# First expert sweep of a mixture layer on Trainium2: tokens' hi and lo parts side by side as one moving operand

## What is computed

```python
def peer(h, w_q, subkeys, u, v):
    ...
        q = (xb @ w_q).reshape(PEER_BLOCK, PEER_HEADS, 2, PEER_DHALF)
        s = jnp.einsum('thpd,hpkd->thpk', q, subkeys).astype(jnp.float32)
        s1, i1 = lax.top_k(s[:, :, 0], PEER_TOPK)
        s2, i2 = lax.top_k(s[:, :, 1], PEER_TOPK)
        ...
        top, pos = lax.top_k(cand, PEER_TOPK)
        idx = jnp.take_along_axis(cidx, pos, axis=-1)
        g = jax.nn.softmax(top, axis=-1)
        ue, ve = u[idx], v[idx]
        act = jax.nn.gelu(jnp.einsum('td,thkd->thk', xb, ue).astype(jnp.float32), approximate=False)
        return jnp.einsum('thk,thkd->td', (g * act).astype(xb.dtype), ve)
```

## Time and profile before

| | us |
|---|---|
| median of 3 runs | 5239.82 |
| lowest, highest | 5237.86, 5244.24 |
| the profiled execution | 5246.08 |
| its span (first to last instruction) | 5244.1 |
| first sweep of peer00: first to last matmul into `dot` | 521.5 to 988.1 |
| the same of peer01 | 1372.5 to 1839.4 |
| the same of peer10 | 2528.4 to 2997.6 |
| TensorE busy in the whole span | 4602.8 |
| VectorE busy | 3384.8 |
| ScalarE busy | 2318.3 |
| GpSimd busy | 1137.3 |

### The profile page before, as it was taken

One profiled execution on the slowest core, in us unless ns is written; L12 is line 12 of the kernel. 1 busy time (PEld: TensorE's weight loads), 2 busy tenths in 40 slices (PEclk: granted clock), 3 DMA queues, 4 the chain that ended last, 5 costly groups with the idle time before them and its releaser, 6 DMA issues. The chain is left out here.

```text
span 5244.1 us, 91248 instructions
## 1 busy us (share of the span) xinstructions
PE 4602.8 (88%) x35718; PEld 4375.4 (83%) x35718; DVE 3384.8 (65%) x5726; ACT 2318.3 (44%) x3890; POOL 1137.3 (22%) x945
## 2 busy tenths in 40 slices
PE   8768999999899999885899999798888979888896
PEld 5546999999899999773899899698777979877796
DVE  6554797688698778725698688555365545446554
ACT  6414544455444445432454454343363434345343
POOL 0000029645105844300017745200000000000000
PEclk9888999999999999997999999899799989978898
DMA  8411686788487678620487688544314535421352
GB/s 294 163 40 46 195 278 213 233 292 297 164 256 237 217 269 296 210 101 22 158 264 224 209 288 297 186 164 150 105 53 137 184 112 174 152 93 63 135 186 94
DMA packets 293104, 950.64 MB, mean 181 GB/s; under 512 B 32592, under 2 KB 84880, under 8 KB 292038
## 3 DMA queue, kind: packets, MB, share of 16 engines
q1 hardware_dynamic: 264070, 841.59, 48.1%
q0 software_dynamic: 28032, 100.82, 5.9%
q10 hardware_dynamic: 576, 2.39, 0.1%
HBM read 899.40 MB, written 45.13 MB: 180 GB/s over the span
## 5 line engine op out<-in xcount | busy, mean ns | idle before, releaser
L150 DVE TENSOR_TENSOR weight_lo<-weight_ring,weight_hi 128x1024 fp32r<-128x1024 f32 x1420 | 1785.0, 1257 | 1295.9 <-ACT weight_hi L145 1291.1
L145 ACT ACTIVATE weight_hi<-weight_ring 128x1024 fp32r<-128x1024 f32 x1420 | 1498.8, 1056 | 1880.4 <-issue 883.7
L177 PE MATMUL ffn_gu<-second_x_hi,weight_hi 128*128 128x256 f32 x1408 | 399.3, 284 | 37.6 <-PEq L209 37.6
L177 PE MATMUL ffn_gu<-second_x_lo,weight_hi 128*128 128x256 f32 x1408 | 398.4, 283 | 0.0
L177 PE MATMUL ffn_gu<-second_x_hi,weight_lo 128*128 128x256 f32 x1408 | 398.4, 283 | 0.0
L177 PE MATMUL peer10e_dot<-peer_xh,weight_hi 128*128 128x224 f32 (+1 forms) x1152 | 325.5, 283 | 8.8 <-DVE weight_lo L150 5.9
L177 PE MATMUL peer01e_dot<-peer_xh,weight_hi 128*128 128x224 f32 (+1 forms) x1152 | 324.4, 282 | 9.2 <-DVE weight_lo L150 6.5
L177 PE MATMUL peer00e_dot<-peer_xh,weight_hi 128*128 128x224 f32 (+1 forms) x1152 | 324.3, 282 | 8.2 <-DVE weight_lo L150 5.6
L177 PE MATMUL peer10e_dot<-peer_xl,weight_hi 128*128 128x224 f32 (+1 forms) x1152 | 318.1, 276 | 0.0
L177 PE MATMUL peer10e_dot<-peer_xh,weight_lo 128*128 128x224 f32 (+1 forms) x1152 | 318.0, 276 | 0.0
L177 PE MATMUL peer00e_dot<-peer_xh,weight_lo 128*128 128x224 f32 (+1 forms) x1152 | 317.4, 275 | 0.0
(11 more groups left out here) (681 smaller groups left out, 14250.2 us busy)
## 6 DMA issues: line engine op xcount, KB each, us to landing
weight_ring<-in_peer_tiles SPq DMA_DIRECT2D x768, 512.0 KB, 4.5
weight_ring<-in_w_tiles SPq DMA_DIRECT2D x652, 512.0 KB, 3.3
peer_acts<-peer00e_gelu SPq DMA_DIRECT2D x64, 224.0 KB, 4.8
peer00e_act_in<-peer_acts SPq DMA_DIRECT2D x64, 224.0 KB, 5.3
peer_acts<-peer01e_gelu SPq DMA_DIRECT2D x64, 224.0 KB, 4.7
peer01e_act_in<-peer_acts SPq DMA_DIRECT2D x64, 224.0 KB, 5.0
peer_acts<-peer10e_gelu SPq DMA_DIRECT2D x64, 224.0 KB, 4.7
peer10e_act_in<-peer_acts SPq DMA_DIRECT2D x64, 224.0 KB, 5.2
```

The costliest lines, as they stand in the source:

```text
L145: act.activation(self.tile_of(self.hi, g), self.ring[:, g % RING, :], ACT.Copy).then_inc(self.hi_done, 2)
L150: dve.tensor_tensor(self.tile_of(self.lo, g), self.ring[:, g % RING, :], self.tile_of(self.hi, g).bitcast(F32), ALU.subtract).then_inc(sel ...
L177: last = pe.matmul(out, lhsT, rhs, start=start and i == 0, stop=stop and i == len(passes) - 1, **more)
```

## The change

The tokens' pair becomes one tensor, `x_pair[P, KD, 2, T]`, with the hi and the lo part of a k-tile next to each other. In the first sweep the two matmuls that use the hi weights become one, whose moving operand is both parts (2 x 256 or 2 x 224 columns) and whose result is 512 or 448 PSUM columns: hi by hi in the left half, lo by hi in the right half. The matmul with the lo weights adds to the left half. The two halves still have to be summed: ScalarE copies the right half out (`half`, into `q` or into a new buffer `joined`), and VectorE adds the left half to it in place (`join`). The gelu reads `joined`, in SBUF. TensorE waits before tile n for `join` of tile n-2 (`joined_done`) where it waited for ScalarE's read. The second sweep is as before.

```diff
             def score(c):
                 ...
-                pe.wait_ge(read_out, c + 1)
+                pe.wait_ge(joined_done, c + 1)
                 ...
                 if half == 0 and n >= 2:
-                    pe.wait_ge(read_out, n - 1)
+                    pe.wait_ge(joined_done, n - 1)
                 cols, width = (slice(0, T), T) if n < QT else (slice(SPARSE, T), DENSE)
                 for k in range(4):
-                    at_k = tuple(b[:, cols] for b in x(4 * half + k))
-                    last = run_passes(pe, dot[:, n % 2, 0:width], W.stationary(2 * q0 + m, k * P, at_k),
-                                      half == 0 and k == 0, half == 1 and k == 3)
+                    part = 2 * q0 + m
+                    w_hi, w_lo = (w[:, part % PARTS, k * P:(k + 1) * P] for w in (W.hi, W.lo))
+                    pe.matmul(dot[:, n % 2, 0:2 * width].rearrange("p (a t) -> p a t", a=2), w_hi, x_pair[:, 4 * half + k, :, cols],
+                              start=half == 0 and k == 0, stop=False, skip_group_check=True)
+                    last = pe.matmul(dot[:, n % 2, 0:width], w_lo, x_pair[:, 4 * half + k, 0, cols], start=False,
+                                     stop=half == 1 and k == 3, skip_group_check=True)
                 last.then_inc(W.used, 1)
...
+            def join(n):
+                dve.wait_ge(half_out, n + 1)
+                width, out = (T, q[:, n % 2, :]) if n < QT else (DENSE, joined[:, n % 2, :])
+                dve.tensor_tensor(out, out, dot[:, n % 2, 0:width], ALU.add).then_inc(joined_done, 1)
...
             for m in range(2 * front):
                 now[0] = m
+                if m % 2:
+                    join(m // 2)
                 W.next_lo(dve, 2 * q0 + m)
...
+            def half(n):
+                act.wait_ge(W.used, 2 * (q0 + n) + 2)
+                if n < QT:
+                    ...
+                    out = q[:, n % 2, :]
+                else:
+                    if n >= QT + 2:
+                        act.wait_ge(read_out, n - QT - 1)
+                    out = joined[:, n % 2, :]
+                width = out.shape[1]
+                act.activation(out, dot[:, n % 2, width:2 * width], ACT.Copy).then_inc(half_out, 1)
+
             for m in range(2 * front):
                 n = m // 2
+                if m % 2:
+                    half(n)
                 W.next_hi(act, 2 * q0 + m)
...
-                    if n < QT:
-                        if n >= 2:
-                            act.wait_ge(scored, n - 1)
-                        act.activation(q[:, n % 2, :], dot[:, n % 2, 0:T], ACT.Copy).then_inc(read_out, 1)
-                    else:
+                    if n >= QT:
                         k = (n - QT) // 2
+                        act.wait_ge(joined_done, n + 1)
                         if k >= 2:
                             act.wait_ge(stored[k % 2], 16 * (k // 2))
-                        act.activation(gelu[:, k % 2, n % 2, :], dot[:, n % 2, 0:DENSE], ACT.Gelu).then_inc(read_out, 1)
+                        act.activation(gelu[:, k % 2, n % 2, :], joined[:, n % 2, :], ACT.Gelu).then_inc(read_out, 1)
```

More of the change, by code:

```diff
@@ L704, with peer_experts @@
 LEAD = 5
-def peer_experts(nc, W, name, layer, x, route, h, gate, const, keys_dram, acts_dram, u_rows, v_rows, x_hi, x_lo, x_at):
+def peer_experts(nc, W, name, layer, x, route, h, gate, const, keys_dram, acts_dram, u_rows, v_rows, x_pair, x_at):
     q0, u0, v0 = (W.take("peer_%s%d" % (kind, layer)) for kind in "quv")
@@ L714, in peer_experts @@
     ident, iota, iota16 = const[:, 0:P], const[:, 2 * P:3 * P], const[:, 3 * P:3 * P + 16]
+    x_hi, x_lo = x_pair[:, :, 0, :], x_pair[:, :, 1, :]
     HC = PH * TOPK
@@ L755, in peer_experts @@
         spread_end = spread_at[0] + 4 * 2 * HOTS * GROUP * P
+        joined = S.sb("joined", [P, 2, DENSE])
         weight = over(spread_at, spread_end, "weight", [P, 2, DENSE])
@@ L773, in peer_experts @@
          second_done, multiplied, spread_out, weighed, hi_done, weighted, twice_done, x_turned, xt_done, picked_done,
-         pick_in, consumed, dotted, shared, folded) = (
+         pick_in, consumed, dotted, shared, folded, joined_done, half_out) = (
             S.sem(n) for n in ("keys_in", "read_out", "scored", "scores_out", "ordered", "exp_in", "exped",
@@ L777, in peer_experts @@
                                "spread_out", "weighed", "hi_done", "weighted", "twice_done", "x_turned", "xt_done",
-                               "picked_done", "pick_in", "consumed", "dotted", "shared", "folded"))
+                               "picked_done", "pick_in", "consumed", "dotted", "shared", "folded", "joined_done", "half_out"))
         stored = [S.sem("stored%d" % i) for i in range(2)]
@@ L1031, in store @@
             def store(k):
-                sync.wait_ge(read_out, QT + 2 * k + 2)
+                sync.wait_ge(read_out, 2 * k + 2)
                 sync.dma_start(acts_dram[k * P:(k + 1) * P, :], gelu[:, k % 2, :, :].rearrange("p a t -> p (a t)")
@@ L1184, in _ @@
                     pe.wait_ge(folded, 1)
-                    pe.wait_ge(read_out, front)
+                    pe.wait_ge(joined_done, front)
                     for n in range(KD):
@@ L1206, in gelu_rows @@
                     act.activation(dots[:, :], dots[:, :], ACT.Gelu).then_inc(dotted, 1)
+            def half(n):
+                act.wait_ge(W.used, 2 * (q0 + n) + 2)
+                if n < QT:
+                    if n >= 2:
+                        act.wait_ge(scored, n - 1)
+                    out = q[:, n % 2, :]
[5 more added lines that the diff above has]
+                act.activation(out, dot[:, n % 2, width:2 * width], ACT.Copy).then_inc(half_out, 1)
             for m in range(2 * front):
                 n = m // 2
+                if m % 2:
+                    half(n)
                 W.next_hi(act, 2 * q0 + m)
@@ L1259, in peer @@
     x_at = -(-nc.sbuf_base // 32) * 32
-    with nc.sbuf_tensor(name + "_xh", [P, KD, T], F32R) as x_hi, nc.sbuf_tensor(name + "_xl", [P, KD, T], F32R) as x_lo, \
+    with nc.sbuf_tensor(name + "_x", [P, KD, 2, T], F32R) as x_pair, \
             nc.sbuf_tensor(name + "_route", [P, 3, T], F32) as route:
-        x = split_pair(x_hi, x_lo)
+        x = split_pair(x_pair[:, :, 0, :], x_pair[:, :, 1, :])
         norm(nc, name + "n", lambda c: h[:, c, :], None, KD, T, const[:, P:2 * P],
@@ L1265, in peer @@
         peer_experts(nc, W, name + "e", layer, x, route, h, gate, const, dram["subkeys%d" % layer], dram["acts"],
-                     dram["u_rows"], dram["peer_tiles"], x_hi, x_lo, x_at)
+                     dram["u_rows"], dram["peer_tiles"], x_pair, x_at)
 def even_mixer(nc, W, h, modulation, scales, cols, const, rope_dram):
```

## The result

The changed kernel took 5253.17 us (median of 7 runs, 5249.26 to 5261.23) beside 5238.9 us for the kernel before in the same session: a ratio of 1.0021, 95% interval 1.0011 to 1.0031, or 11 us. Measured again on another chip it was 1.0018 (1.0009 to 1.0027). The profiled execution of after took 5250.4 us, its span 5248.4.

A forecast was written before the change was run, and what follows sets the result against it. VectorE's list of work was taken to bound routing, TensorE the queries, GpSimd the spreading. Terms -5.1 + 28.3 + 2.4 - 12 + 1.0 = +14.6 us, on 5239.8, gave 5254.4 us, range 5226 to 5294.

The forecast's parts named there:

- turn: End of routing: TensorE's new wait for join delays the transposes by 0.8 us a sweep, +2.4 us in all.
- end of the sweep: Start of the second sweep: the last gelu is stored behind half, +0.34 us, +1.0 for three sweeps.
- TensorE's pace: First-sweep matmuls: an expert k-group falls from 0.334 to 0.311 us, saving 0.20 us a tile; query tiles save 0.107.
- join: VectorE: each join lasts about 0.38 us and adds 0.30 us, bounds 0.26 and 0.38.
- with 1 us for leftover gaps: Routing stretch: VectorE bounds it end to end, 207.0 against 196.8 us with 1 us of gaps; three sweeps +28.3 us.
- a sign that would make the forecast wrong: Routing stretch: the granted clock falling below 1.00, where TensorE will have longer gaps.
- GpSimd limits it: Spreading stretch: GpSimd's 12.4 us of idle time is the most it can give; -4 us a sweep, -12 for three.
- 1: Whole kernel: TensorE sets the pace everywhere and join is hidden; together -81, 5159 us; chance 0.08.
- 2: Spreading stretch: GpSimd gives way, so the full 11.6 us is gained there; 5230 us; chance 0.10.
- 3: Spreading stretch: join behind the one-hots stalls tile n+2, taking back the gain and 2 us more; 5272 us; chance 0.13.
- 4: TensorE: no gain, by the skill page's pace rule or a slower 448-wide matmul; 5272 us; chance 0.07.
- 5: Spreading stretch: join holds GpSimd up as the lo part does, 18 us a sweep, +54 more; 5308 us; chance 0.07.

The follow-up runs named there:

- Experiment 8: The changed kernel with one more join-sized VectorE addition, result unused, for each of tiles 17 to 84 (routing stretch): 5304.5 us, 1.0105 of the kernel before.
- experiment 5: The changed kernel with ScalarE copying both halves, VectorE adding the copies, TensorE waiting for the copy, not join: 5283.94 us, 1.0064 of the kernel before.
- experiment 9: The changed kernel with ScalarE's gelu of a tile one step later, behind the next hi part: 5242.19 us, 0.9987 of the kernel before.
- Experiment 1: The changed kernel with its wide matmul made two narrow ones again, half and join kept: 5301.24 us, 1.0105 of the kernel before.
- experiment 3: The changed kernel with join moved behind the lo part of tile n+3: 5441.15 us, 1.037 of the kernel before.
- experiment 7: The changed kernel with one more join-sized VectorE addition per tile from 86 on (spreading stretch), result unused: 5270.48 us, 1.0041 of the kernel before.

## Why the prediction was right, and where its terms were not

The time came 1 us from the forecast of 5254.4; by the ratios, which compare with the kernel before of the same session, the change was +11 and +9 us where +14.6 was forecast. In the routing stretch, which sets the sign, the mechanism was the forecast one; in the spreading stretch it was not. The closeness is partly luck, since a loss that was forecast too small cancels gains that were forecast too small.

| term, three sweeps, us | forecast | measured, first profile |
|---|---|---|
| queries and routing | -5.1 + 28.3 = +23.2 | +32.8 |
| turn | +2.4 | +4.4 |
| spreading | -12 | -21.6 |
| end of the sweep | +1.0 | -6.8 |
| sum | +14.6 | +8.8 |

**TensorE's pace: right.** A wide and a narrow matmul take 0.313 us together, 851.36 to 851.67 in the timeline of after, against the 0.311 worked out; for 512 and 256 columns it is 0.35 against 0.347. The rule by which the prediction saw no gain, columns at 2.4 GHz plus 2.5 ns, was the wrong one to take from the Trainium skill: the section that it cites, "Back-to-back issue gap" of "TensorE: Matmul & The Clock Gate", gives it for an isolated matmul and says itself that a stream of weight loads and matmuls runs otherwise, with 81 ns at 128 columns and 131 ns at 512. This trace has 111 and 227, so neither rule holds here, and the pace has to come from rows. For the queries the stretch is 57.0 to 55.6 us, -1.4 where -1.7 was forecast.

**join: right.** 0.375 us long, 0.30 to the next start, 0.306 in VectorE's sum.

**Routing: the step that was mis-sized is "with 1 us for leftover gaps".** VectorE's work is 205.28 us, where 206.0 was forecast, and it has 5.3 us of gaps (210.60 - 205.28). I filled its idle time as if it could be used anywhere, but it idles at single places, and a join elsewhere cannot use that. Eight waits for hi parts, 3.1 us above, and one for `half`, 0.7 us, are in the trace; the rest of the gaps I can't place. Experiment 8 used up about half of the 5 us, experiments 5 and 9 (without TensorE's wait for join, and with the gelu later) none to speak of. Why the hi parts came late at those places was not tested.

**Turn: right in kind, and more in size.** In peer01 the turn grew by 1.0 us where 0.8 was forecast, and in peer10 by 0.9. In peer00 it grew by 2.4, and there the granted clock is low after the change and was not before. Two windows of after around it, columns as above (the third number from the end is the granted clock), and two matmul pairs:

```profile
780.60:783.90 3.30, 3.30 (x14) 3.06 (x13) 3.27 (x7) 1.02 (x2) 0.96 (x1) 0.51 0.65 214
785.00:786.40 1.40, 1.40 (x11) 1.33 (x10) 0.95 (x1) 0.62 (x2) 0.00 (x0) 1.00 0.75 247
```

```profile
779.76 0.45 PE L1169 MATMUL peer00e_dot<-peer_x,weight_hi 128*128 128x448 f32 x1 [2.23 <-DVE peer00e_joined L985]
...
781.45 0.60 PE L1169 MATMUL peer00e_dot<-peer_x,weight_hi 128*128 128x448 f32 x1
...
782.04 0.60 PE L1169 MATMUL peer00e_dot<-peer_x,weight_hi 128*128 128x448 f32 x1
```

After a wait of 2.23 us the granted clock is at 0.51, 1.2 GHz, for 3.3 us, and a pair takes 0.59 us instead of 0.31. This was named as a sign that would make the forecast wrong; it is there, but costs only about 1.4 us where it comes. After the same wait in peer01 it did not come; in peer10 it came in both kernels, in the kernel before after a wait of 1.73 us. In the profile of the second measurement it came in all three sweeps, in that of experiment 9 in one, each time after 2.2 us of waiting.

**Spreading: the step that failed is "GpSimd limits it".** The stretch follows TensorE: 0.166 us (8 x (0.334 - 0.313)) for each of the 58 tiles in it is 9.6 us, and 7.2 came. TensorE's waits went from 5.4 us for GpSimd to 4.2 us for the copy of `G` and 1.7 us for join. Summed over TensorE's steps from one start to the next in peer00, those with a wait take 7.0 us before, 9.3 in after and 4.2 in experiment 9, and all others 205.7, 195.8 and 196.2: that is the whole stretch, and without the circle of experiment 9 the gain is 11.9. GpSimd's idle time, which I took for the most it could give, went up from 9.3 to 27.0 us while the stretch got shorter, since its one-hots fell from 1437 to 1187 ns; from the first to the last of them it is now 187.6 us, and not 191. Experiment 1 separates the two: with narrow matmuls GpSimd has 38.8 us of idle time, and the stretch is as long as before the change. TensorE no longer waits for GpSimd there, and 5.1 us for the copy of `G` and for join have come in its place. GpSimd's busy time was not work but partly time lost beside VectorE, and that depends on what VectorE does next to it. GpSimd counts where it is nearly full, with the 5.4 us of TensorE's waits before the change and 7.7 in experiment 5, and it does not set the length of the stretch. Why join leaves the one-hots shorter is shown in part: with join in front of the lo part they take 1187 ns, with a join of 8 columns there 1452, with join behind the lo part 1401. That fits the 0.3 us by which the full join puts the lo part later; that the lo part then falls where GpSimd waits anyway is only argued.

**End of the sweep: wrong sign.** The first fetch was issued later after the last matmul, as forecast, but it landed sooner. GpSimd's first use of it, in before and in after, with the issue ahead of it:

```profile
990.05 0.93 SPq L1041 DMA_DIRECT2D peer00e_act_in<-peer_acts  x2
...
995.69 1.27 POOL L1088 TENSOR_TENSOR peer00e_weight<-peer00e_act_in,peer00e_G 128x224 f32<-128x224 f32 x2 [5.27 <-DMA peer00e_act_in<-peer_acts]
```

```profile
994.28 0.92 SPq L1050 DMA_DIRECT2D peer00e_act_in<-peer_acts  x2
...
997.09 1.27 POOL L1097 TENSOR_TENSOR peer00e_weight<-peer00e_act_in,peer00e_G 128x224 f32<-128x224 f32 x2 [1.67 <-DMA peer00e_act_in<-peer_acts]
```

5.6 us from issue to use against 2.8. Experiments 1, 3 and 7 have gaps of 9.5 to 10.8 us like before, all the others 6.9 to 8.2; what decides it was not tried. One thing goes with it in all profiles: GpSimd issues the fetch of the last gathered rows shortly before SyncE's fetch, and in the 12 sweeps with a long gap those rows have landed before GpSimd can use SyncE's fetch (at 7.1 us after the last matmul's end in peer00 before, where the use is at 7.4), in the 30 with a short one they land after it (9.4 and 5.2 in after). Whether that is the cause is open.

**The rivals.** 1 fell (TensorE idles 27 us in the routing stretch). 2 was right that GpSimd gives way; what came is 2.4 us short of TensorE's own 9.6, since the steps with a wait grew by 2.3. 3 named the place, the one-hots ahead of join, and underrated the exit: not tile n+2 but the copy of `G` was late, and it took 4.7 us of the gain and did not turn it into a loss. 4 fell by the pace. 5 fell: the one-hots got shorter and not longer.

## What to carry to other kernels

A change that moves work from a full engine to another one has a sign for each stretch, so cut the kernel where the bound changes and apply it only where the receiving engine has room: here that turned +0.2% into -0.7%. When an instruction gets a new wait, list what stands behind it on its own queue, and put it behind what others need: the gelu one step later gave 4.7 us a sweep more. Idle time counts as room only where it lies, and an engine's busy time that holds stalls from a neighbour is no bound.

## What was not expected of the hardware

GpSimd's one-hot of the same shape took 1131, 1187, 1437 and 1564 ns on average in experiment 1, in after, in before and in experiment 5, with other work of VectorE beside it; the shortest single one took 781 ns in after and in experiment 5. A matmul of 448 columns and one of 224 in turn start 0.21 and 0.105 us apart, though each 224-wide one in a row of its kind needs 0.111. After a wait of 2.23 us the granted clock went down to 0.51 in two of the three sweeps and not in the third; in the second measurement, after waits of the same length, in all three. Over the profiles of all runs it went to its lower level at this place in 4 of 15 sweeps after waits of 1.7 us, in 16 of 24 after waits of 2.0 to 2.2 us, and in none of the three of experiment 8, after waits of 2.5 us. So the length of the wait alone does not decide it.
